# Encoder trunk in split fp32 on one core: four score tiles in a row, fewer constant products, three held units, and a moved weight piece

## The reference

```
layer 0: h = gelu(x @ a_w_in); u, v = split(h); v = layernorm(v)
         mixed over 128 positions by a_w_s (8 groups); h = (u * mixed) @ a_w_out
layer 1: q, k, v = split(x @ b_w_qkv)          # 8 heads, two 64-wide q/k halves j each
         p_j = softmax(q_j k_j^T / 8 + bias);  attn = p_0 - lam * p_1;  o = attn @ v
         o = o * rsqrt(mean(o^2) + eps) * g;   h = o @ b_w_out
each:    x = layernorm(1.41 * x + h)
         gate, up = split(x @ f_w_in); h = (gelu(conv3(gate)) * up) @ f_w_down
         x = layernorm(1.41 * x + h)
```

## Time and profile before

| what | value |
|---|---|
| median of three runs | 1278.77 us (1278.75 to 1279.49) |
| profiled execution | 1278.82 us |
| its span, first to last instruction | 1277.1 us |
| TensorE busy | 1266.7 us, 99% |
| VectorE busy | 650.4 us, 51% |
| ScalarE busy | 459.2 us, 36% |
| POOL busy | 164.9 us, 13% |

### The profile page before, as it was taken

How to read it: one execution, slowest core, us unless ns; L and a number is a source line. 1 busy time by engine, 2 the same in 40 slices (tenths; PEclk the granted TensorE clock), 3 DMA queues, 4 the chain that set the end, 5 groups by cost and what they waited for, 6 DMA issues and landing times.

```text
span 1277.1 us, 15677 instructions
## 1 busy us (share of the span) xinstructions
PE 1266.7 (99%) x6104; PEld 1056.8 (83%) x6104; DVE 650.4 (51%) x889; ACT 459.2 (36%) x553; POOL 164.9 (13%) x159
## 2 busy tenths in 40 slices
PE   9999999999999999999999999999999999999997
PEld 8888888889888888888888877788988888888886
DVE  3637877346343434433372777775653334343346
ACT  3422333322232323322314588775143222232230
POOL 3001100040000000000224444443100000000001
PEclk9999999999999999999999999999999999999999
DMA  8434554250322232222522334324033333322221
GB/s 263 151 96 123 173 175 148 90 183 3 130 99 99 90 101 80 98 92 97 193 71 74 102 100 122 95 104 168 30 99 99 99 99 99 99 99 99 99 99 66
DMA packets 104507, 140.62 MB, mean 110 GB/s; under 512 B 9424, under 2 KB 81192, under 8 KB 104208
## 3 DMA queue, kind: packets, MB, share of 16 engines
q1 hardware_dynamic: 94880, 127.68, 31.0%
q0 software_dynamic: 9440, 12.11, 2.9%
q10 hardware_dynamic: 144, 0.26, 0.1%
HBM read 137.85 MB, written 10.52 MB: 116 GB/s over the span
## 4 chain that ended last, share of the span: by engine, by line
PE 97%; DVE 2%; ACT 0%; issue 0%; POOL 0%; DVEq 0%; POOLq 0%
PE bank L1261 31%; PE bank L1265 31%; PE bank L1264 31%; PE bank L1643 1%; PE bank L1497 1%; PE bank L1271 1%; PE bank L1395 1%; PE bank L1421 0%; DVE x_tok L819 0%; DVE r_stat L788 0%; PE bank L1386 0%; PE bank L1500 0%; DVE x_tok L810 0%; DVE x_tok L782 0%; DVE w_lo L870 0%
## 5 line engine op out<-in xcount | busy, mean ns | idle before, releaser
L1261 PE MATMUL bank<-xt_hi,w_hi 128*128 128x512 f32 (+1 forms) x1008 | 380.8, 378 | 0.0
L1265 PE MATMUL bank<-xt_hi,w_lo 128*128 128x512 f32 (+1 forms) x1008 | 378.8, 376 | 0.0
L1264 PE MATMUL bank<-xt_lo,w_hi 128*128 128x512 f32 (+1 forms) x1008 | 378.7, 376 | 0.0
L760 DVE TENSOR_TENSOR w_lo<-w_raw,w_hi 128x2048 fp32r<-128x2048 f32 x79 | 180.8, 2289 | 184.6 <-ACT w_hi L466 158.3
L1261 PEld LDWEIGHTS bank<-xt_hi,w_hi 128*128 128x128 f32 x1008 | 189.7, 188 | 36.5 <-issue 3.0
L1265 PEld LDWEIGHTS bank<-xt_hi,w_lo 128*128 128x128 f32 x1008 | 189.7, 188 | 34.6
L1264 PEld LDWEIGHTS bank<-xt_lo,w_hi 128*128 128x128 f32 x1008 | 189.8, 188 | 33.7
L466 ACT CAST w_hi<-w_raw 128x2048 fp32r<-128x2048 f32 x53 | 101.2, 1912 | 186.2 <-PE bank L1261 185.1
L1261 PE MATMUL bank<-w_hi,s_hi 128*128 128x512 f32 x416 | 162.2, 390 | 0.6 <-POOL w_lo L1874 0.6
L1265 PE MATMUL bank<-w_hi,s_lo 128*128 128x512 f32 x416 | 161.9, 389 | 0.0
L1264 PE MATMUL bank<-w_lo,s_hi 128*128 128x512 f32 x416 | 161.8, 389 | 0.0
(11 more groups left out here) (209 smaller groups left out, 1490.3 us busy)
## 6 DMA issues: line engine op xcount, KB each, us to landing
w_raw<-in_f_w_in_dram SPq DMA_DIRECT2D x44, 1024.0 KB, 5.1
w_raw<-in_f_w_down_dram SPq DMA_DIRECT2D x22, 1024.0 KB, 4.8
w_raw<-in_a_w_in_dram SPq DMA_DIRECT2D x14, 1024.0 KB, 5.8
bias_by_query_key<-bias_by_distance POOLq DMA_DIRECT2D x8, 1024.0 KB, 15.9
w_raw<-in_a_w_out_dram SPq DMA_DIRECT2D x8, 1024.0 KB, 6.7
w_raw<-in_b_w_qkv_dram SPq DMA_DIRECT2D x16, 512.0 KB, 4.7
bias_sb<-bias_by_query_key SPq DMA_DIRECT2D x32, 256.0 KB, 2.6
w_raw<-in_b_w_qkv_dram SPq DMA_DIRECT2D x4, 1024.0 KB, 5.3
```

Of the source, the lines that this page charges most:

```text
L760: dve.tensor_tensor(lo_of(u), w_raw[:, u % 2, :], hi_of(u), ALU.subtract).then_inc(w_lo_done, 1)
L1261: ins = pe.matmul(o, a_hi, b_hi, start=start, stop=False)
L1264: pe.matmul(o, a_hi, b_lo, start=False, stop=False)
L1265: return pe.matmul(o, a_lo, b_hi, start=False, stop=stop)
```

## The change

At the start 10 constant products run in place of 20, and 3 in place of 6. In the head loop the four score tiles of heads 1 to 7 run in one row, behind a part of the projection and ahead of all values; tile 2 moves to banks 5 and 6, and tile 3 to banks 2 and 3, where it waits for VectorE to have read tile 0. VectorE's order follows: scores 0 to 2, sums of tile 0, score 3, and the mixes after all scores. In the last head POOL makes piece 3 of a weight unit ahead of share 2 instead of behind it. In the last output projection three units are held; tiles 0 and 1 take all three, then tiles 2 and 3 half by half. VectorE finishes each tile before it begins the next, and the last tile is scaled and stored in three parts (512, 256 and 256 columns).

```diff
-        def score_bank(t, j):
-            return bank[(1, 4)[j] if t % 2 else 2 + j]
+        def score_bank(h, t, j):
+            if h == 0:
+                return bank[(1, 4)[j] if t % 2 else 2 + j]
+            return bank[((2, 3), (1, 4), (5, 6), (2, 3))[t][j]]
...
-            sp.wait_ge(out_stored, 16 * (TB + 1))
+            sp.wait_ge(tail_ready, 3)
+            sp.dma_start(ov[TB - 1, :, D - 2 * P:D], x_tok[:, TB - 1, D - 2 * P:D]).then_inc(out_stored, 16)
+            sp.wait_ge(out_stored, 16 * (TB + 2))
...
+            values_hi(TB + 2)
             exps(h + 1, 0)
-            values_hi(TB + 2)
...
                 probs_lo(h, 2)
+                probs_lo(h, 3)
                 scored(h + 1, 0)
-                probs_lo(h, 3)
                 scored(h + 1, 1)
+                scored(h + 1, 2)
                 weighed(h + 1, 0)
+                scored(h + 1, 3)
                 weighed(h + 1, 1)
-                scored(h + 1, 2)
                 mixed(h + 1, 0)
-                scored(h + 1, 3)
                 mixed(h + 1, 1)
...
             scored(h + 1, 0)
-            probs_lo(h, 3)
+            values_lo(TB + 2)
             scored(h + 1, 1)
+            scored(h + 1, 2)
             weighed(h + 1, 0)
-            values_lo(TB + 2)
+            scored(h + 1, 3)
             weighed(h + 1, 1)
-            scored(h + 1, 2)
             mixed(h + 1, 0)
-            scored(h + 1, 3)
             stationary(o_t, S_BO, 0)
...
+            for t in range(TB):
+                for h in range(2):
+                    add_half(n, t, h)
+                    stats_half(n, t, h)
                 moments(n, t)
-                centre(n, t)
-                add_half(n, t + 1, 0)
-                scale(n, t).then_inc(rows_ready, 1)
...
+                if t < TB - 1:
+                    centre(n, t)
+                    scale(n, t).then_inc(rows_ready, 1)
...
-            for h in range(2):
-                scale(n, t, slice(NB * h, NB * h + NB), h + 1).then_inc(tail_ready, 1)
+            scale(n, t, slice(0, NB), 1).then_inc(tail_ready, 1)
+            scale(n, t, slice(NB, D - 2 * P), 2).then_inc(tail_ready, 1)
+            scale(n, t, slice(D - 2 * P, D), 2).then_inc(tail_ready, 1)
...
+                held = 3 if e is None else 2
+                loops = (n - 1 - held) // 2
...
                 if e is None:
+                    out_ready(u0, s0, n - 3)
+                    out_unit(u0, n - 3, (0, 1), frees=1)
+                    out_ready(u0, s0, n - 2)
+                    out_unit(u0, n - 2, (0, 1))
+                    out_ready(u0, s0, n - 1)
+                    out_unit(u0, n - 1, (0, 1), stop=True)
                     for t in range(2, TB):
-                        out_unit(u0, n - 2, (t,))
-                        out_unit(u0, n - 1, (t,), stop=True)
+                        for h in range(2):
+                            out_unit(u0, n - 3, (t,), halves=(h,))
+                            out_unit(u0, n - 2, (t,), halves=(h,))
+                            out_unit(u0, n - 1, (t,), stop=True, halves=(h,))
...
-            constant_products(20)
+            constant_products(10)
...
-                    constant_products(6)
+                    constant_products(3)
...
-                        pe.wait_ge(sc_done, 2 * TB * (h - 1) + 5)
+                        pe.wait_ge(sc_done, 2 * TB * (h - 1) + (5 if h == 1 else 7))
...
+                    else:
+                        pe.wait_ge(sc_done, 2 * TB * h)
+                if t == 2 and h:
+                    pe.wait_ge(at_lo_done, TB * h)
                 for j in range(2):
-                    n = 2 * TB * h + 2 * t + j
-                    if n >= 4:
-                        pe.wait_ge(sc_done, n - 3)
+                    if h == 0 and t >= 2:
+                        pe.wait_ge(sc_done, 2 * t + j - 3)
+                    elif t == 3:
+                        pe.wait_ge(sc_done, 2 * TB * h + j + 1)
...
                 turn_probs(h, 3)
-                scores(h + 1, 0)
-                scores(h + 1, 1)
                 project(h + 2, 0, range(3, 6))
-                values(h, 0)
-                values(h, 1)
-                scores(h + 1, 2)
-                scores(h + 1, 3)
-                values(h, 2)
-                values(h, 3)
+                for t in range(TB):
+                    scores(h + 1, t)
+                for k in range(TB):
+                    values(h, k)
...
-            scores(h + 1, 0)
-            scores(h + 1, 1)
             value_pair(U_V67, 1)
-            scores(h + 1, 2)
-            scores(h + 1, 3)
+            for t in range(TB):
+                scores(h + 1, t)
...
+                if h == H - 1:
+                    piece(u, 3)
                 shares(h, 2)
-                piece(u, 3)
+                if h < H - 1:
+                    piece(u, 3)
                 shares(h, 3)
```

More of the change, by code:

```diff
@@ L747, in _ @@
             act_e.wait_ge(tail_ready, 2)
-            act_e.dma_start(out[0].rearrange("(t p) d -> t p d", p=P)[TB - 1, :, NB:D], x_tok[:, TB - 1, NB:D]
+            act_e.dma_start(out[0].rearrange("(t p) d -> t p d", p=P)[TB - 1, :, NB:D - 2 * P],
+                            x_tok[:, TB - 1, NB:D - 2 * P]
                             ).then_inc(out_stored, 16)
@@ L1116, in scored @@
                     dve.wait_ge(sc_mm, 2 * TB * h + 2 * t + j + 1)
-                    dve.tensor_tensor_reduce(prob[:, t, j, :], score_bank(t, j)[:, :], bias_sb[:, t, :], -1.0, 3.0e38,
+                    dve.tensor_tensor_reduce(prob[:, t, j, :], score_bank(h, t, j)[:, :], bias_sb[:, t, :], -1.0, 3.0e38,
                                              ALU.add, ALU.min, nmax[:, t, j:j + 1]).then_inc(sc_done, 1)
@@ L1349, in outward @@
             def outward(u0, n, s0, e, first=1):
-                loops = (n - 3) // 2
+                held = 3 if e is None else 2
+                loops = (n - 1 - held) // 2
                 if loops > 1:
@@ L1357, in outward @@
                             out_unit(u0, j, range(TB), frees=1)
-                for j in range(first + (2 * loops if loops > 1 else 0), n - 2):
+                for j in range(first + (2 * loops if loops > 1 else 0), n - held):
                     out_ready(u0, s0, j)
                     out_unit(u0, j, range(TB), frees=1)
[L1361 to L1366, removed]
-                if e is None:
+                if e is None:
+                    out_ready(u0, s0, n - 3)
[4 more added lines that the diff above has]
+                    out_unit(u0, n - 1, (0, 1), stop=True)
                     for t in range(2, TB):
-                        out_unit(u0, n - 2, (t,))
-                        out_unit(u0, n - 1, (t,), stop=True)
-                else:
+                        for h in range(2):
+                            out_unit(u0, n - 3, (t,), halves=(h,))
+                            out_unit(u0, n - 2, (t,), halves=(h,))
+                            out_unit(u0, n - 1, (t,), stop=True, halves=(h,))
+                else:
+                    out_ready(u0, s0, n - 2)
+                    out_unit(u0, n - 2, (0,), frees=1)
+                    out_ready(u0, s0, n - 1)
+                    out_unit(u0, n - 1, (0,), stop=True)
+                    out_unit(u0, n - 2, (1,))
+                    out_unit(u0, n - 1, (1,), stop=True)
                     out_unit(u0, n - 2, (2, 3))
@@ L1623, in scores @@
                         pe.wait_ge(bv_lo_done, TB)
+                    else:
+                        pe.wait_ge(sc_done, 2 * TB * h)
+                if t == 2 and h:
+                    pe.wait_ge(at_lo_done, TB * h)
                 for j in range(2):
-                    n = 2 * TB * h + 2 * t + j
-                    if n >= 4:
-                        pe.wait_ge(sc_done, n - 3)
+                    if h == 0 and t >= 2:
+                        pe.wait_ge(sc_done, 2 * t + j - 3)
+                    elif t == 3:
+                        pe.wait_ge(sc_done, 2 * TB * h + j + 1)
                     r = slice(HD * j, HD * j + HD)
                     q = slice(t * P, t * P + P)
-                    product(score_bank(t, j)[:, :], qk_hi[r, h % 2, 0, q], qk_lo[r, h % 2, 0, q],
+                    product(score_bank(h, t, j)[:, :], qk_hi[r, h % 2, 0, q], qk_lo[r, h % 2, 0, q],
                             qk_hi[r, h % 2, 1, :], qk_lo[r, h % 2, 1, :], True, True).then_inc(sc_mm, 1)
@@ L1718, in _ @@
             out_ready(U_BO, S_BO, 0)
-            pe.wait_ge(sc_done, 2 * TB * (H - 1) + 6)
+            pe.wait_ge(sc_done, 2 * TB * H)
             out_unit(U_BO, 0, (1,), start=True, frees=1)
```

14 lines of the change are left out of this document (1 added, 13 removed).

## The result

The kernel after takes 1283.49 us (median of 10 runs, 1281.71 to 1284.95) against 1279.15 (10 runs, 1278.62 to 1279.66): ratio 1.0034, interval 1.0026 to 1.0042. It is slower by 4.3 us. The forecast was 1278.4 with a range up to 1281.3, so the time lies outside the range and on its slow side.

A forecast was written before the change was run, and what follows sets the result against it. TensorE, busy 1266.7 of 1277.1 us, was taken as the bound. Start -1.25, end -1.05, tail 0, six heads +1.0 and last head +0.95 sum to -0.35, giving 1278.4 us after a 0.05 median correction; range 1272.6 to 1281.3.

The forecast's parts named there:

- the last head: Last pass of the head loop: block and old wait saved, bank, piece and value split lost; about +0.95 us.
- later slack: Last head: 0.2 us counted among the savings, beside the block's -0.43 and the old wait's -0.69.
- Six heads: Six passes of the head loop with merged scores: +0.17 us a head, +1.0 in all.
- Tile 3's bank: Score block: tile 3 reuses tile 0's banks, which VectorE releases late; +0.40 us a head.
- the mean square's wait: Each looped head: TensorE's mean square waits 0.1 us for query's low part and reloads; +0.20 us.
- switch: Changing between full and score products: one block of four tiles in place of two saves 0.43 us a head.
- POOL gets in first: Six heads: POOL's share precedes VectorE's mix and square, query's low part 0.9 us later; +5.4, 1283.8 us; chance 0.13.
- Nothing waits: Head loop and last head: no waits at all, tile 3's bank included; -6.0, 1272.8 us; chance 0.12.
- no queue: Heads: VectorE and POOL do not queue and the mean square finds its operand; -3.0, 1275.8 us; chance 0.20.
- Start: Program start: fewer constant products let the first real product start about 1.25 us earlier, kept to the end; -1.25.
- the rival of the clock: Start: TensorE's clock rises late because it idled ahead of the full products; +1.5, 1279.9 us; chance 0.07.
- End: Last output projection: VectorE's add begins 1.05 us earlier, directly after the last product; -1.05 us.

The follow-up runs named there:

- e7: Kernel after with the last value split ahead of mix 3 in VectorE's order in the last head; 1280.83 us, ratio 1.0013.
- e2: Kernel before with only the four score tiles in one row, with their banks and VectorE's and ScalarE's order; 1282.52 us, ratio 1.0028.
- e6: Kernel after with all four of POOL's weight pieces ahead of share 0 in heads 1 to 7; 1278.36 us, ratio 0.9993.
- e8: Kernel after with all POOL pieces ahead of its shares and the last value split ahead of mix 3; 1278.1 us, ratio 0.9991.
- e1: Kernel before with only the fewer constant products, 10 for 20 and 3 for 6; 1279.13 us, ratio 0.9999.
- e10: Kernel before with 11 constant products ahead of the first transposes, six behind them as before; 1279.23 us, ratio 1.0002.
- e12: Kernel after with POOL's pieces first, the value split ahead of mix 3, and the old 20 and 6 constant products; 1277.85 us, ratio 0.999.
- e11: Kernel before with 40 constant products ahead of the first transposes, six behind them as before; 1283.68 us, ratio 1.0035.
- e3: Kernel before with only the new end: three held units, VectorE's order, last tile in three scales and two stores; 1278.08 us, ratio 0.9993.
- e4: Kernel before with only POOL's piece 3 moved ahead of share 2 in the last head; 1278.31 us, ratio 0.9996.
- e5: Kernel before with the merged scores and POOL's piece 3 ahead of share 2, start and end as before; 1283.95 us, ratio 1.004.

## Why the prediction was wrong

**The failed step is the last head, +0.95 forecast, +3.55 measured: mix 3 counted at its plain length, and the clock behind the wait not counted.** Three stretches of TensorE, from the pass's second transposes on, place it (before; after):

| stretch | before | after | difference | forecast |
|---|---|---|---|---|
| second transposes to the output product | 15.25 | 14.91 | -0.34 | -0.32 |
| output product to the first value product | 2.85 | 5.45 | +2.60 | +1.3 |
| first value product to the last head's transposes | 1.44 | 2.72 | +1.28 | 0 |

In the second stretch I took mix 3 at its plain length, although POOL's next weight unit starts there: that unit was not in my count at all. Mix 3 took 1.74 us. The value split came at 860.32 where my count gave about 859.3 (its own 15.45, from a block start at 843.84): 1.0 us. The 0.2 that I had booked as later slack did not show either. e7 shows that the split's place behind mix 3 is the cause, for with the split ahead of it the wait is gone; e2 shows what lengthens the mix, for with the unit 1.2 us behind its start it took 0.75.
My order was wrong too, but that cost nothing. I let share 1 in between mix 0 and the stationary low part. VectorE ran the two back to back (851.11 and 851.93), and the share took 2.18 us and ended 1.0 later than counted. Piece 3 and mix 1, counted at 11.1 and 11.7 behind the block's start, ended at 11.03 and 11.58 all the same, and share 3 at 14.10 instead of 14.2.
In the third stretch the clock fell to the 1.2 GHz level, which I had not counted at all: 1.2 us within the pass, 0.17 behind it; the remaining 0.1 also stands in e7 (1.52 against 1.44).
The fall does not come in every execution, it seems. The ten times of the kernel after form two groups, four at 1281.7 to 1282.0 and six at 1283.2 to 1285.0, and the mean granted clock of each execution splits in the same way: 0.998 in all four, 0.997 in all six. A fall of 3.4 us to half takes 0.0013 off that mean. It is no proof, since the mean varies between 0.998 and 0.999 in the kernel before and no trace of one of the four was taken. Even the four lie above my range, so the clock alone did not make the forecast wrong.

**Six heads, +1.0 forecast, +2.3 measured: mechanism right, size off.** Tile 3's bank (0.40 forecast; block 3.40 against 3.38, second product 0.32 late) came as counted. e6 leaves this in and takes the mean square's wait away: a pass is then 19.53 against 19.48 before, so switch and late bank together cost +0.05 where I had -0.43 + 0.40 = -0.03. The rest, 0.34 a head, is the mean square's wait, for which I had 0.20: it showed at s + 10.59 and I had s + 10.50, and its first product lost another 0.08. Six times 0.22 makes the 1.3 us. By the rows this wait has two parents: POOL's own order (share 1 behind a piece) and the turns with VectorE; e6 removes both together. The skill's rule of the shared port (the Trainium skill, "SBUF — State Buffer", 🔬 SBUF: two separate sides), that such operations exclude each other, agrees with these rows: 1.13 us for a share beside a mix and 0.69 alone, 1.76 for a mix beside a piece.

**Rivals.** "POOL gets in first" gave 1283.8, close to the measured 1283.5, but for another reason: it put 0.9 us in each head, and 0.39 was there. Its place of loss was wrong: 3.55 us lie in the last head. That its number came out is luck. "Nothing waits" and "no queue" have both fallen: even with the mean square's wait taken away (e8) a pass is not shorter than before, so the 0.43 of the second switch is paid back by the late bank. The rows of the kernel after bear this out: tile 3's products take 0.89 us for two steps of 0.23, 0.43 too much. No run parts the two, since one block of scores with banks enough for all its tiles was not tried.

**Start, -1.25 forecast, -0.73 in the profile, 0.0 in the median of e1.** Here the rival of the clock, to which I gave 0.07, held. The first full product does start earlier, by 1.74 us, more than my 1.25, and the wait ahead of it was 0.58 us where I had about 1. In the medians of e1, e10 and e12 nothing of it is left; in e1 a late transfer of x took 0.38 us too, which I had not expected. I had also read the rise before as lying anywhere up to 10.54; the product at 9.13, already at 0.40 us, shows that it had come by then, and e1's products reach that length only at 12.69. In e1's profile the transposes at 10.55 are slow, in e10's those at 10.00 are fast. What decides when the clock rises stays open; e11 excludes only that the constant products do it. That the idle time ahead of the first product is to blame, as the rival had it, is not shown. The Trainium skill ("TensorE: Matmul & The Clock Gate", Part 1) says that activity lifts the level; the trace agrees in part only, for in e11 TensorE was busy for 8.8 us with constant products and was still at the lower level.

**End, -1.05 forecast, -0.74 in the profile, -0.9 in e3.** The add did move by 1.05 us. My 0 for the tail was the error: 0.14 came back up to the last issue (a third scale, and a second store 0.39 behind the first) and 0.17 behind it, for the 128 KB landed in 2.2 us, no sooner than the 256 KB before (2.1).

**POOL's piece** is worth the wait that it removes beside the old scores (-0.7 in e4) and harms beside the merged ones (+1.4 from e2 to e5). The cost came one step later, at the value split: the early piece lets the output product run early, with it ScalarE's high part of the next unit, and with that POOL's pieces, which now meet mix 3 (1.0 of the 1.4 us). I had seen that wait and its direction, but took the sum of the last head as one number and did not ask what it would be without the piece.

## What to carry to other kernels

A small engine off the critical path can decide a step: before moving work on VectorE or GpSimd, put both engines' two-input operations of that stretch on one time line, the next weight unit's too, and let an operation that finds the other engine at work begin its own time only when that one is done (a mix beside a piece took 1.74 to 1.77 us instead of 0.74); then place the waiting engine's long work where the other reads one of its inputs from PSUM (the value split at 859.64 kept its 0.68 us beside a piece) or idles. Ask also what an earlier operation sets off: here a piece moved forward brought the next unit forward into a mix. A merged block saves one change of mode, but the bank that it needs again sooner can cost as much, so count the release against the need before counting the switch. Where a change may open a wait on TensorE of the size seen here (2.4 us), allow for half speed behind it too (1.4 us here).

## What the runs showed of the hardware

- The granted clock fell to 0.50 with idle stretches of 2.41 us (after: during the wait) and 2.43 us (e5: 1.2 us behind it) between products, and did not fall in e2's profile, where TensorE waited 1.94 us. Both falls lasted 3.4 us. The mean granted clocks of the other executions suggest that the same wait does not bring a fall each time.
- Forty 128-column constant products in a row (8.8 us of full occupation) did not lift the clock at the start; it had risen by 16.16 us, with full products between the transposes from 11.75 on. While the transposes took 1.07 us the granted clock was still shown as full, so at the start the duration of a known instruction is the only sign.
- In the last head a GpSimd operation that waited for VectorE did not get in between two VectorE operations with two SBUF inputs, although it was issued before the second (851.44 against 851.93): it took 2.18 us, where it takes 0.69 alone. e2, e5 and e7 show the same row (2.18 to 2.19).
- Two stores of 128 KB took 2.1 and 2.2 us to land, one of 256 KB 2.1.
